# Both differences of each recurrence level on GpSimd, with a third exponential buffer

## The reference, cut to what matters

```python
f = lb + (1.0 - lb) * jax.nn.sigmoid(f_logit)
k = 1.0 - f
bc = jnp.cumsum(log f)                       # b, along the tokens of a chunk
inter = einsum('bhtk,bhkv->bhtv', q * exp(b), state)
rel = where(causal, b[t] - b[s], -inf)
att = einsum('bhtk,bhtsk,bhsk->bhts', q, exp(rel), k)
intra = einsum('bhts,bhsv->bhtv', att, v)
new_state = exp(b_last) * state + einsum('bhsk,bhsv->bhkv', k * exp(b_last - b), v)
```

## Time and profile before

| | |
|---|---|
| median of 3 runs | 2142.43 us (2141.09 to 2143.94) |
| the profiled execution's own time | 2144.7 us |
| its span, first to last instruction | 2143.0 us |
| mean granted TensorE clock | 0.973 |
| busy over the span: PE, PEld, DVE, ACT, POOL | 93%, 80%, 76%, 61%, 30% |
| the recurrence, in us from the span's start | 376 to about 497 |

### The profile page before, as it was taken

One profiled execution on the slowest core, in us unless ns is written; L12 is line 12 of the kernel. 1 busy time (PEld: TensorE's weight loads), 2 busy tenths in 40 slices (PEclk: granted clock), 3 DMA queues, 4 the chain that ended last, 5 costly groups with the idle time before them and its releaser, 6 DMA issues. The chain is left out here.

```text
span 2143.0 us, 40176 instructions
## 1 busy us (share of the span) xinstructions
PE 1999.7 (93%) x11184; PEld 1716.0 (80%) x11185; DVE 1622.1 (76%) x2205; ACT 1314.2 (61%) x1896; POOL 639.1 (30%) x743
## 2 busy tenths in 40 slices
PE   7999978788985999999999999999999999999993
PEld 6887867676874979889798898978898888978882
DVE  5343166895656978889888898889898898988985
ACT  5221244663444766867767676677777676776765
POOL 3100000320234232524425244244324253342521
PEclk9999989999986999999999999999999999999997
DMA  5222120004245988989899898989898898988988
GB/s 187 58 79 69 42 96 1 11 21 144 89 151 188 366 283 275 317 266 370 264 323 310 274 362 259 340 298 371 268 345 291 292 339 264 355 281 301 333 258 308
DMA packets 264158, 506.40 MB, mean 236 GB/s; under 512 B 37708, under 2 KB 38732, under 8 KB 263778
## 3 DMA queue, kind: packets, MB, share of 16 engines
q1 hardware_dynamic: 242984, 457.79, 61.5%
q0 software_dynamic: 21120, 47.90, 8.8%
HBM read 466.38 MB, written 39.22 MB: 236 GB/s over the span
## 5 line engine op out<-in xcount | busy, mean ns | idle before, releaser
L1841 DVE TENSOR_TENSOR wlo<-raw,whi 128x1024 fp32r<-128x1024 f32 x774 | 950.3, 1251 | 74.3 <-ACT whi L1320 71.7
L1320 ACT ACTIVATE whi<-raw 128x1024 fp32r<-128x1024 f32 x775 | 844.6, 1116 | 159.4 <-PE ps L1008 104.0
L1006 PE MATMUL ps<-xT,whi 128*128 128x320 f32 x1920 | 502.2, 348 | 0.6
L1008 PE MATMUL ps<-xT,wlo 128*128 128x160 f32 x1920 | 454.9, 237 | 0.0
L1008 PEld LDWEIGHTS ps<-xT,wlo 128*128 128x128 f32 x1920 | 367.6, 191 | 0.6
L1006 PEld LDWEIGHTS ps<-xT,whi 128*128 128x128 f32 x1920 | 361.5, 188 | 4.1 <-ACT y L1355 3.5
L640 PE MATMUL ps<-whi,xT 128*128 128x512 f32 x544 | 217.5, 400 | 0.0
L642 PE MATMUL ps<-whi,xT 128*128 128x512 f32 x544 | 214.2, 394 | 0.0
L641 PE MATMUL ps<-wlo,xT 128*128 128x512 f32 x544 | 213.6, 393 | 0.0
L640 PE MATMUL ps<-whi,aT 128*128 128x512 f32 x512 | 210.5, 411 | 0.3 <-DVE aTl L1902 0.3
L642 PE MATMUL ps<-whi,aTl 128*128 128x512 f32 x512 | 200.9, 392 | 0.0
(11 more groups left out here) (311 smaller groups left out, 3577.0 us busy)
## 6 DMA issues: line engine op xcount, KB each, us to landing
raw<-in_w SPq DMA_DIRECT2D x780, 512.0 KB, 9.2
raw<-in_w_in SPq DMA_DIRECT2D x16, 512.0 KB, 4.8
xs<-in_x SPq DMA_DIRECT2D x8, 512.0 KB, 10.2
raw<-in_w_out SPq DMA_DIRECT2D x8, 512.0 KB, 3.7
mix<-in_x SPq DMA_DIRECT2D x8, 512.0 KB, 4.2
acc_d<-mix SPq DMA_DIRECT2D x8, 512.0 KB, 5.1
h_d<-h SPq DMA_DIRECT2D x8, 512.0 KB, 2.6
mix<-acc_d SPq DMA_DIRECT2D x8, 512.0 KB, 7.7
```

What stands on the lines that cost most here:

```text
L1006: pe.matmul(o2, wh[:, a, cols], xT2[:, :, k, 0:JOB_T], start=q == 0 and a == 0, stop=False, skip_group_check=True)
L1008: m = pe.matmul(o, wl[:, a, cols], xT2[:, 0, k, 0:JOB_T], start=False, stop=q == QUARTERS - 1 and a == 1, skip_group_check=True)
L1320: act.activation(parted(slot(whis, s)), paired(raw_slot(s), s), ACT.Copy).then_inc(split_hi, 1)
L1841: dve.tensor_tensor(parted(slot(wlos, s)), paired(raw_slot(s), s), parted(slot(whis, s).bitcast(F32)), ALU.subtract).then_inc(split_lo, 1)
```

## The change

VectorE's `args` goes away altogether. GpSimd makes both differences of a level one after the other and reports the level once, by `arg_set`; `arg_low` no longer exists. The exponentials have three buffers: the two of `he` and a third, `he3`, in the place of `hgs`. So GpSimd at levels 0 to 6 and ScalarE at steps 7 and 8 wait for the products of step s - 3 rather than s - 2. Ahead of its loop GpSimd waits until the staging row has been written out. The order of VectorE's products and copies stays as it was.

```diff
+    he3 = at("he3", R[0] - 4 * KB, [P, T])
...
+        def exps_of(s):
+
+            return (he[:, 0, :], he[:, 1, :], he3[:, :])[s % 3]
...
                     act.wait_ge(arg_set, args_by(s))
-                    act.wait_ge(arg_low, args_by(s))
-                    act.activation(he[:, s % 2, :], he[:, s % 2, :], ACT.Exp).then_inc(exp_set, 1)
+                    act.activation(exps_of(s), exps_of(s), ACT.Exp).then_inc(exp_set, 1)
...
-                    act.wait_ge(prod_dve, dve_prods_by(s - 2))
+                    act.wait_ge(prod_dve, dve_prods_by(s - 3))
...
-            def args(s):
-
-
-                hd, L = divmod(s, STEPS)
-                e = he[:, s % 2, :]
-                b = hf[:, hd, :]
-                if s >= 2:
-                    dve.wait_ge(prod_dve, dve_prods_by(s - 2))
-                if L < LEVELS:
-                    h = 64 >> L
-                    bv, ev = (z.rearrange("p (m two h) -> p m two h", two=2, h=h) for z in (b, e))
-                    mid = bv[:, :, 0, h - 1:h].broadcast_to([P, T // (2 * h), h])
-                    dve.tensor_tensor(ev[:, :, 1, :], bv[:, :, 1, :], mid, ALU.subtract).then_inc(arg_set, 1)
...
             for s in range(STEPS * HH + 2):
-                if s < STEPS * HH:
-                    args(s)
                 if 1 <= s <= STEPS * HH:
                     prods(s - 1)
...
             pool.wait_ge(sums_set, HH)
+            for i in range(2):
+                pool.wait_ge(hg_out[i], 64)
             for s in range(STEPS * HH):
                 hd, L = divmod(s, STEPS)
                 if L < LEVELS:
                     h = 64 >> L
-                    if s >= 2:
-                        pool.wait_ge(prod_dve, dve_prods_by(s - 2))
-                    bv, ev = (z.rearrange("p (m two h) -> p m two h", two=2, h=h)
-                              for z in (hf[:, hd, :], he[:, s % 2, :]))
-                    pool.tensor_tensor(ev[:, :, 0, :], bv[:, :, 0, h - 1:h].broadcast_to([P, T // (2 * h), h]),
-                                       bv[:, :, 0, :], ALU.subtract).then_inc(arg_low, 1)
+                    if s >= 3:
+                        pool.wait_ge(prod_dve, dve_prods_by(s - 3))
+                    bv, ev = (z.rearrange("p (m two h) -> p m two h", two=2, h=h) for z in (hf[:, hd, :], exps_of(s)))
+                    mid = bv[:, :, 0, h - 1:h].broadcast_to([P, T // (2 * h), h])
+                    pool.tensor_tensor(ev[:, :, 0, :], mid, bv[:, :, 0, :], ALU.subtract)
+                    pool.tensor_tensor(ev[:, :, 1, :], bv[:, :, 1, :], mid, ALU.subtract).then_inc(arg_set, 1)
```

More of the change, by code:

```diff
@@ L305, in build @@
             sem(n) for n in ("reset_set", "keys_set", "logs_set", "sums_set", "keys_out", "keys_in"))
-        arg_low = sem("arg_low")
         arg_set, exp_set, prod_dve, diag_done, level_used, level_copied = (
@@ L1231, in _ @@
                 elif L == LEVELS:
-                    act.wait_ge(prod_dve, dve_prods_by(s - 2))
+                    act.wait_ge(prod_dve, dve_prods_by(s - 3))
                     for t in range(NT):
-                        m = act.activation(he[:, s % 2, t * P:(t + 1) * P], hf[:, hd, t * P:(t + 1) * P], ACT.Exp,
+                        m = act.activation(exps_of(s)[:, t * P:(t + 1) * P], hf[:, hd, t * P:(t + 1) * P], ACT.Exp,
                                            scale=-1.0, bias=hf[:, hd, t * P + P - 1:t * P + P])
@@ L1238, in _ @@
                 else:
-                    act.wait_ge(prod_dve, dve_prods_by(s - 2))
-                    act.activation(he[:, s % 2, :], hf[:, hd, :], ACT.Exp).then_inc(exp_set, 1)
+                    act.wait_ge(prod_dve, dve_prods_by(s - 3))
+                    act.activation(exps_of(s), hf[:, hd, :], ACT.Exp).then_inc(exp_set, 1)
                     act.wait_ge(level_used, used_by(STEPS * hd + LEVELS))
@@ L1613, in prods @@
                     ov, qv, ev = (z.rearrange("p (m two h) -> p m two h", two=2, h=h)[:, :, 1, :]
-                                  for z in (hp[:, s % 2, :], hq[:, hd, :], he[:, s % 2, :]))
+                                  for z in (hp[:, s % 2, :], hq[:, hd, :], exps_of(s)))
                     dve.tensor_tensor(ov, qv, ev, ALU.mult)
                     ov, kv, ev = (z.rearrange("p t (m two h) -> p t m two h", two=2, h=h)[:, :, :, 0, :]
-                                  for z in (by_tile(hp[:, s % 2, :]), key_cols(hd), by_tile(he[:, s % 2, :])))
+                                  for z in (by_tile(hp[:, s % 2, :]), key_cols(hd), by_tile(exps_of(s))))
                     dve.tensor_tensor(ov, kv, ev, ALU.mult).then_inc(prod_dve, 1)
                 elif L == LEVELS:
-                    dve.tensor_tensor(by_tile(hp[:, s % 2, :]), key_cols(hd), by_tile(he[:, s % 2, :]),
+                    dve.tensor_tensor(by_tile(hp[:, s % 2, :]), key_cols(hd), by_tile(exps_of(s)),
                                       ALU.mult).then_inc(prod_dve, 1)
                 else:
-                    dve.tensor_copy(decay[:, :], he[:, s % 2, :].rearrange("p (t n) -> p t n", n=P)[:, :, P - 1])
-                    link(dve.tensor_tensor(hpx[:, :], hq[:, hd, :], he[:, s % 2, :], ALU.mult))
+                    dve.tensor_copy(decay[:, :], exps_of(s).rearrange("p (t n) -> p t n", n=P)[:, :, P - 1])
+                    link(dve.tensor_tensor(hpx[:, :], hq[:, hd, :], exps_of(s), ALU.mult))
                     dve.sem_inc(prod_dve, 1)
```

## The result

The changed kernel takes 2145.80 us (median of 12 runs, 2144.17 to 2149.20), the kernel before beside it 2143.86 (12 runs, 2141.09 to 2145.18). The ratio is 1.0016 with a 95% interval of 1.0009 to 1.0023, so 1.9 to 4.9 us slower. That is within the band of no change by 0.2%, and inside the range, but on the other side of zero than the forecast of -1.5 us.

The account below looks back on a forecast made before the run. VectorE was taken to set the recurrence's pace, excluding GpSimd when both read SBUF. First head +1.6, later heads -1.05, -1.05, -1.0 gave -1.5 us: 2141.0 us median, from 2142.4, range 2136 to 2147.

Parts of the forecast that it names:

- 1.44 us an exchange: Recurrence: a GpSimd operation then a VectorE one, each reading two SBUF tiles, take turns at 0.55 - 0.15 + 1.04 us.
- (a): Rival for the recurrence: no exclusion in the new arrangement, VectorE rid of 4.2 us a head; 2131.5 us, chance 0.07.
- (b): Rival for the recurrence: exclusion milder than the numbers used, -3.1 to -3.2 us, both together 2137.5; chance 0.12.
- (c): Rival for the recurrence: GpSimd keeps the port over its pair, a product waits up to 2.1 us; 2145.8, chance 0.11.
- Rival (d): Contested GpSimd operations, fourteen a head, cost more: +2.5 us at 1.11 us each, +5.8 at 1.17; chance 0.10.
- the three numbers: Port prices: VectorE ends 0.55 us after GpSimd; GpSimd ends 1.04 after a point 0.15 before VectorE's end; exchange 1.44.
- the 26.7 of a head: One later head laid out: VectorE's own 20.6 us, 4.7 of port delays, 1.4 of waiting; 27.8 laid out for before.
- The order at the turn: Where one head passes to the next: GpSimd's pairs were placed from the product that frees each one's buffer.
- The stand behind a copy: Masked copies out of PSUM: 0.86 us each, copy and its wait, counted as VectorE's own work, three a head.
- The price of the upper difference on GpSimd: The moved operation was priced like the lower difference of L2042: 1.03 us alone, 1.04 after a hand-over.
- The first head: First head of the recurrence: 8.6 us of delays against 4.7 in a later head; first state +1.6 us later.
- The clock: TensorE's clock in the recurrence: first standing grows to about 4.7 us, others stay near 2 or under; nothing booked.

Follow-up runs that it names:

- e1: The changed kernel with only two exponential buffers, the third taken away: 2154.6 us, ratio 1.0051 to the kernel before.
- e3: The changed kernel with GpSimd waiting at level 2 for the products of step s - 2, so VectorE's two products go first: 2145.3 us, ratio 1.0008.
- e9: The kernel before with VectorE no longer waiting at once for its masked copies, nothing else changed: 2141.6 us, ratio 1.0002.
- e6: The changed kernel with VectorE no longer waiting at once for its masked copies; the next copy waits instead: 2139.5 us, ratio 0.9987.
- e10: The kernel before with the third buffer and masked copies not waited for at once, VectorE still making upper differences: 2138.8 us, ratio 0.9985.
- e11: The changed kernel with VectorE making the upper differences of the first head as before; a single run: stage 119.9 us.
- e2: The kernel before with the third exponential buffer only, VectorE still making the upper differences: 2141.0 us, ratio 0.9995.
- e4: The changed kernel with both GpSimd differences replaced by write-only memsets, so results are wrong: stage 109.9 us, total 2217.9 us in one run.

## Why the prediction was wrong

**Right.** That the two engines exclude each other, with these prices: 1.44 us an exchange was met again (380.15 to 381.59), and products of 1.5 us fill the profile. That removing VectorE's 23.5 us would gain nearly nothing, and that the third buffer carries the change (e1). Five half-width products a head last 1.5 us (I had said four), and GpSimd's 56 operations have a mean of 1.21 us (I had said 1.15). The rivals without exclusion (a) and with a milder one (b) fell; so did (c), a port held over GpSimd's pair: the product at 380.65 ends at 382.17, 0.54 behind GpSimd's first operation, which ends at 381.63, and the second ends only at 383.14. Rival (d), a dearer operation on GpSimd, had a part, as told below.

**The step that failed: "Then I placed GpSimd's pairs by the three numbers", the 26.7 of a head.** Measured 28.2 and 27.9. Two things in it were wrong, and one price.

*The order at the turn.* I let the first product of level 0 start ahead of GpSimd, unblocked. Rows 5 already had GpSimd at 404.31 and VectorE at 404.32, and GpSimd was first again, by 0.08. Put right, with nothing else changed, the same laying-out gives 27.5 a head, an estimate: the 26.7 and the 0.8 of one blocked product. e3 shows the products free when the order is turned, though what GpSimd then loses takes back more than half of it.

*The stand behind a copy.* I charged 0.86 us from a copy to the next operation and took it as VectorE's own time, the same before and after. Before, it was free in the middle levels, since the operation behind it was L1599, which had to wait for the port anyway (e9: the edit moves the middle level by nothing, and the whole stage by 1.8 us where it moves the changed kernel's by 6.1). After, that operation is a product, 0.93 behind the copy, and GpSimd's operations come first. (The product waits for two semaphores where the difference waited for one; that this makes the 0.07 is likely, but not tested.) e6 and e10 give the stand its price: of the move's 4.0 us of stage 3.5 go with it.

*The price of the upper difference on GpSimd.* I took it for the operation of L2042 with its 1.03 or 1.04. It has its operands the other way round, and its time differs from level to level and is the same in every head to 0.02, with no VectorE operation beside it that reads two SBUF tiles:

```profile
438.71 1.15 POOL L2032 TENSOR_TENSOR he<-hf 128x512 f32<-128x512 f32 x1
...
442.72 1.27 POOL L2032 TENSOR_TENSOR he<-hf 128x512 f32<-128x512 f32 x1
442.99 1.55 DVE L1604 TENSOR_TENSOR hp<-hq,he 128x512 f32<-128x512 f32 x1 [0.21 <-DVE attT L1625]
```

These are levels 3 and 4; levels 0 and 1 take 1.06 and 1.07, level 2 takes 1.11 (in e3, where it is undisturbed), levels 5 and 6 take 1.05. The lower difference takes 1.04 at every level. The mean of a head's 14 operations is 1.07 or 1.08, half of the way from 1.04 to the 1.11 that I priced under rival (d) at +2.5, 4.0 us over the forecast. By the rows the dearer operation matters where a product waits for its end: that of 442.99 ends 0.55 after it, 0.23 later than with 1.04.

The second period (437.56 to 465.46) can be read term by term beside my sum. The port delays eight operations by 5.5 us, where I had 4.7: the blocked product at the turn is the difference. Every one of the eight operations that follow something VectorE waits for itself (states, diagonal, five copies, step 8's product) comes 0.06 to 0.08 later than I had it, 0.55 in all. VectorE stands 1.2 us for other engines, where I had 1.4. So 26.7 + 0.85 + 0.55 - 0.2 = 27.9.

**The first head** was seen in kind and mis-sized: +1.6 laid out, +2.79 measured. e11 gives back all of it but 0.06; against e2, which has the third buffer as e11 has, 0.55 stays, and e11 still has the two products of 1.50 and 1.58 at the first turn. The same two errors are in my sum: both kernels laid out anew, it is +2.4, an estimate. Of the other 0.4 some 0.3 may be the upper differences of levels 2, 3 and 4, 0.07, 0.11 and 0.24 dearer than 1.04, while every operation is held up by the other engine's.

**The clock.** I booked nothing. At the stage's start it fell for longer, to 0.66 from 380 to 390 (before 0.71 and then 0.94), but VectorE hardly stood there. In the changed kernel it fell once more, at the first head's turn:

```profile
400.00:405.00 5.00, 2.88 (x24) 2.45 (x23) 4.64 (x5) 0.93 (x2) 3.84 (x4) 1.00 0.00 0
405.00:410.00 5.00, 4.79 (x28) 4.79 (x29) 4.74 (x6) 3.10 (x4) 3.08 (x4) 0.66 0.00 0
```

The state's products L825 took 3.16 us there, where a head later, at full clock, they took 1.83:

```profile
405.21 3.16 PE L825 MATMUL ps<-hv,kbT 128*128 128x128 f32 x14 [1.17 <-ACT kbT L1248]
...
412.50 0.69 DVE L1604 TENSOR_TENSOR hp<-hq,he 128x512 f32<-128x512 f32 x1 [0.57 <-PE ps L808]
...
433.42 1.83 PE L825 MATMUL ps<-hv,kbT 128*128 128x128 f32 x14 [1.18 <-ACT kbT L1248]
```

The stands of TensorE ahead of it were 1.84, 1.16 and 1.17 us, shorter than those ahead of the other two falls of this trace (4.55 and 2.83), so my "near 2 or under" was no protection. Behind the states VectorE then stood 0.57 us for TensorE, where it stood 0.21 for itself a head later; these 0.36 us cover the first period's 28.21 against 27.90. Why the clock fell at this turn and not at the next stays open.

**The sum.** +2.79 + 0.29 - 0.04 - 0.54 and 0.15 behind the last state are +2.65 of stage, and the interval of the total, 1.9 to 4.9 us, holds it. From the runs the same +2.65 splits into -1.3 for the third buffer (e2), +0.5 for the move without the stands behind copies (e10, e6) and +3.5, what the same move costs more where VectorE stands behind its copies. The last period, of which I expected -1.0, gave -0.54; no run says why.

## What to carry to other kernels

Work that reads SBUF, moved from VectorE to GpSimd, does not relieve VectorE's two-input operations by its own length: count the reads of both engines as one queue, and move what will lie beside VectorE's reads of PSUM. Lay out such a queue with each engine's start to 0.05 us, by the order that the trace shows, since who is second waits until the other's operation is done. Take the price of an operation from a row with the same operands in the same places. And a self-wait that costs nothing may be hidden behind the very operation that the change removes; look at what comes after it before calling it neutral.

## What the runs showed of the hardware

A copy of 128x8 numbers from SBUF to SBUF (L1613) takes 0.17 us alone, but had a mean of 0.61 us in the changed kernel and 0.50 in e4, where GpSimd only wrote: unlike the products, such a copy is held up by GpSimd's writes too. By the Trainium skill ("SBUF — State Buffer", Who interferes with whom) copies can enter a mode with two ports, and such an instruction contends with GpSimd; the trace agrees.

GpSimd's subtraction of 128x512 numbers took 1.04 us at every level with the broadcast operand first. With the broadcast operand second it took 1.06, 1.07, 1.11, 1.15, 1.27, 1.05 and 1.05 us at levels 0 to 6, blocks of 64 tokens down to 1, alike to 0.02 in all heads of the changed kernel, counted from the hand-over where a VectorE operation held it up, and in e1 and e3 where none did.

TensorE's granted clock fell to a mean of 0.66 in a 5 us stretch behind stands of no more than 1.84 us each, in one head and not in the next with nearly the same pattern; so two profiles of nearly equal kernels can differ by some 0.3 us a head for this alone.

The start of the stage wanders by 3.3 us between profiled executions (373.41 to 376.73). Differences of a stage under 3 us are read from the stage's own length, and from totals only where many runs agree.
